# A two-block transformer kernel on one core: the latent edge of the MLA layer rebuilt, and the token reordering moved into the last chunks of the second feed-forward block

## The reference

```python
def _mla_mixer(h_lat, h_ctx, cos, sin, w_in, q_norm, kv_norm, w_uq, w_ukv, q_gain, k_gain, w_out, with_ctx_out):
    cq_l, ckv_l, kr_l = _split_cols(h_lat @ w_in, (512, 256, 32))
    ckv_c, kr_c = _split_cols(h_ctx @ w_in[:, 512:], (256, 32))
    k_l, v_l = keys_values(ckv_l, kr_l, True)     # rms, @ w_ukv, rms per head, rotary on the last 32
    k_c, v_c = keys_values(ckv_c, kr_c, False)
    q = queries(cq_l, True)                        # rms, @ w_uq, rms per head, rotary
    return attention(q, concat(k_c, k_l), concat(v_c, v_l)) @ w_out

xl = xl + mod_l[2] * y_lat
xl = xl + mod_l[5] * _conv_ffn(_modulate(xl, mod_l[3], mod_l[4]), ...)
# second block, first layer
h = rms_norm(x, norm_mix_pre[0], 1e-6)
m = hybrid_mixer(h, ...)    # differential and dilated window attention
```

## Time and profile before

| | us |
|---|---|
| median of 3 runs | 3988.12 (3987.25 to 3989.57) |
| profiled execution | 3985.7 |
| its span | 3983.7 |
| PE busy | 3752.9 (94%) |
| DVE busy | 1608.4 |
| ACT busy | 1514.2 |
| POOL busy | 1266.9 |

### The profile page before, as it was taken

How to read it: one execution, slowest core, us unless ns; L and a number is a source line. 1 busy time by engine, 2 the same in 40 slices (tenths; PEclk the granted TensorE clock), 3 DMA queues, 4 the chain that set the end, 5 groups by cost and what they waited for, 6 DMA issues and landing times.

```text
span 3983.7 us, 56653 instructions
## 1 busy us (share of the span) xinstructions
PE 3752.9 (94%) x21520; PEld 2948.7 (74%) x21520; DVE 1608.4 (40%) x2348; ACT 1514.2 (38%) x2528; POOL 1266.9 (32%) x524
## 2 busy tenths in 40 slices
PE   6998999999987989999979999989998999998998
PEld 3865678888865655788857778868876777876886
DVE  2423454242326664433355553331136555223113
ACT  3324442121245554322355553332235555333222
POOL 2530043222231010344522223434442222343443
PEclk9999999999998999999989999999999999999999
DMA  4344422111220000222311112222231211222232
GB/s 184 114 172 161 175 91 68 64 63 64 69 80 22 17 22 33 84 95 100 106 53 64 64 64 80 95 74 95 97 103 59 64 64 64 80 95 74 95 99 85
DMA packets 84717, 333.98 MB, mean 84 GB/s; under 512 B 9520, under 2 KB 9648, under 8 KB 78000
## 3 DMA queue, kind: packets, MB, share of 16 engines
q1 hardware_dynamic: 83808, 329.22, 24.3%
q10 hardware_dynamic: 720, 2.10, 0.2%
HBM read 329.18 MB, written 2.10 MB: 83 GB/s over the span
## 4 chain that ended last, share of the span: by engine, by line
PE 62%; issue 25%; POOL 5%; DVE 4%; ACT 2%; POOLq 0%; DVEq 0%; ACTq 0%
PE pB L2097 13%; PE pB L274 12%; PE pB L276 12%; PE pB L275 12%; POOL w_lo L2652 5%; PE pS L2127 1%; PE pT L2155 1%; PE pT L1706 1%; PE pB L1680 1%; PE pS L424 1%; PE pO L2177 1%; PE pO L2182 1%; PE pS L1697 1%; PE pO L276 1%; PE pO L274 1%
## 5 line engine op out<-in xcount | busy, mean ns | idle before, releaser
L2652 POOL TENSOR_TENSOR w_lo<-w_raw,w_hi 128x1024 fp32r<-128x1024 f32 x520 | 1266.7, 2437 | 2691.7 <-ACT w_hi L316 2691.1
L274 PE MATMUL pB<-h_hi,w_hi 128*128 128x512 f32 (+1 forms) x2112 | 839.1, 397 | 72.6 <-DVE h_lo L2581 20.1
L275 PE MATMUL pB<-h_lo,w_hi 128*128 128x512 f32 (+1 forms) x2112 | 830.1, 393 | 0.0
L276 PE MATMUL pB<-h_hi,w_lo 128*128 128x512 f32 (+1 forms) x2112 | 829.6, 393 | 0.0
L316 ACT ACTIVATE w_hi<-w_raw 128x1024 fp32r<-128x1024 f32 x520 | 547.6, 1053 | 477.8 <-PE pB L276 317.4
L274 PEld LDWEIGHTS pB<-h_hi,w_hi 128*128 128x128 f32 x2112 | 402.6, 191 | 174.8 <-issue 59.5
L276 PEld LDWEIGHTS pB<-h_hi,w_lo 128*128 128x128 f32 x2112 | 402.0, 190 | 85.1
L275 PEld LDWEIGHTS pB<-h_lo,w_hi 128*128 128x128 f32 x2112 | 402.9, 191 | 82.3 <-issue 0.5
L274 PE MATMUL pB<-b_hi,w_hi 128*128 128x512 f32 (+1 forms) x1088 | 399.7, 367 | 1.2 <-POOL w_lo L2652 0.9
L276 PE MATMUL pB<-b_hi,w_lo 128*128 128x512 f32 (+1 forms) x1088 | 397.2, 365 | 0.0
L275 PE MATMUL pB<-b_lo,w_hi 128*128 128x512 f32 (+1 forms) x1088 | 397.2, 365 | 0.0
(11 more groups left out here) (510 smaller groups left out, 5173.6 us busy)
## 6 DMA issues: line engine op xcount, KB each, us to landing
w_raw<-stream SPq DMA_DIRECT2D x520, 512.0 KB, 3.3
under<-ada SPq DMA_DIRECT2D x42, 1024.0 KB, 4.9
arena<-ada SPq DMA_DIRECT2D x6, 1024.0 KB, 18.8
x<-xT SPq DMA_DIRECT2D x1, 2048.0 KB, 10.1
out<-x SPq DMA_DIRECT2D x8, 256.0 KB, 2.0
xc<-cT SPq DMA_DIRECT2D x1, 1024.0 KB, 11.0
arena<-bmask ACTq DMA_DIRECT2D x1, 1024.0 KB, 4.8
arena<-brope ACTq DMA_DIRECT2D x2, 256.0 KB, 5.9
```

The source lines that it names most:

```text
L274: pe.matmul(dst, lh, rh, start=(begin and k == 0), stop=False)
L275: pe.matmul(dst, lh, rl, start=False, stop=False)
L276: last = pe.matmul(dst, ll, rh, start=False, stop=(end and k == len(pairs) - 1))
L2652: pool.tensor_tensor(w_lo[:, s, :], w_raw[:, s, :], w_hi[:, s, :].bitcast(F32), ALU.subtract).then_inc(lo_ready, 1)
```

## The change

Two edits at once.

1. MLA entry. The order of norms becomes `cq`, `ckv_lat`, `ckv_ctx`. The context norm is made by strips between the chunks 2 to 4; the squares and sums of `cq` lie around chunk 6, those of `ckv_lat` and `ckv_ctx` before and after the last context chunk. `act_mla_in` is one list of evacuations, squares, roots and hi tiles. `cq` goes to the upper half of pair B, and some buffers of the heads move between H and B; the attention outputs of pairs 4 to 7 go to H. In `FIRST_TURNS` Q and K of head 1 come before C, and PE waits for `ckv_ctx` only at C. In odd pairs the rotary step moves from step 4 to step 6 and the weight split from step 4 to step 5.

2. Reordering. In the last piece of the feed-forward block DVE writes residual plus old `x` to a buffer (`permuted_body`), ACT copies it with the stride into `x` and squares it for `mixpre0`, which becomes a norm by strips (`act_permute`, `pe_out_sums` through `sums="mixpre0"`). `dve_permute` and the norm's own squares and sums are gone.

```diff
-NORMS = [..., "cq", "ckv_ctx", "ckv_lat", "mla_ffn"]
+NORMS = [..., "cq", "ckv_lat", "ckv_ctx", "mla_ffn"]
-        STRIPS = ["ffn_lat", "ffn_ctx", "mla_lat", "mla_ffn"] + [...]
+        STRIPS = ["ffn_lat", "ffn_ctx", "mla_lat", "mla_ctx", "mla_ffn", "mixpre0"] + [...]
@@ pe_ffn / act_ffn / dve_ffn
+            sums = sums or post
...
-                if post is None or p + 1 < len(PIECES):
+                if p + 1 < len(PIECES):
                     act_out(act, g0 + 2 * nj)
+                elif post is None:
+                    act_permute(act, g0 + 2 * nj)
...
-                items(dve, KD, SLOTS, lambda m: out_body(p, g0 + 2 * nj, m))
+                if last_body is not None and p + 1 == len(PIECES):
+                    for m in range(KD):
+                        last_body(g0 + 2 * nj, m)
+                else:
+                    items(dve, KD, SLOTS, lambda m: out_body(p, g0 + 2 * nj, m))
@@ heads
-        hsq_q = [under[:, 2 + b, 6 * T:7 * T] for b in range(2)]
-        hsq_l = [under[:, 2 + b, 7 * T:8 * T] for b in range(2)]
+        hsq_q = [under[:, b, 6 * T:7 * T] for b in range(2)]
+        hsq_l = [under[:, b, 3 * T:4 * T] for b in range(2)]
-        q_src = (h_hi[:, 2 * TC:], h_lo[:, 2 * TC:])
+        q_src = (b_hi[:, KD * C:], b_lo[:, KD * C:])
+        def o_place(p):
+            return B if p < PAIRS_A // 2 else H
-        FIRST_TURNS = [("Q", 0), ("K", 0), ("C", 0), ("SQ", 0), ("SK", 0), ("SC", 0), ("Q", 1), ("K", 1), ("SQ", 1), ("SK", 1)]
+        FIRST_TURNS = [("Q", 0), ("K", 0), ("Q", 1), ("K", 1), ("SQ", 0), ("SK", 0), ("C", 0), ("SC", 0), ("SQ", 1), ("SK", 1)]
+                if turn == ("C", 0):
+                    pe.wait_ge(nlo_ready, norm_done("ckv_ctx"))
-                    if p + 1 < PAIRS_A and p % 2 and s == 4:
+                    if p + 1 < PAIRS_A and p % 2 and s == 5:
                         act_hi_part(act, g + 6)
-                        if s == (4 if p % 2 else 6):
+                        if s == 6:
                             dve_turn(dve, ("rotary", 2 * p + 3))
@@ pe_mla_in
-            pe_first_chunks(pe, G_MLA[0], 2, normed("mla_lat"), H, T, T)
-            pe_norm(pe, "mla_ctx", C)
-            items(pe, 5, SLOTS, lambda m: pe_chunk(pe, m + G_MLA[0], H, T, T), 2)
-            pe.wait_ge(nlo_ready, norm_done("mla_ctx"))
-            items(pe, 3, SLOTS, lambda m: pe_chunk(pe, m + G_MLA[1], B, C, C))
+            pe_first_chunks(pe, lat, 2, normed("mla_lat"), H, T, T)
+            pe_strip_sums(pe, "mla_ctx", 0, 4, C)
+            chunk(2)
+            pe_strip_sums(pe, "mla_ctx", 4, KD - 1, C)
+            chunk(3)
+            pe_strip_end(pe, "mla_ctx", C)
+            chunk(4)
+            chunk(5)
+            for kt in range(2):
+                pe_square_sum(pe, "cq", kt, T)
+            chunk(6)
+            for kt in range(2, 4):
+                pe_square_sum(pe, "cq", kt, T)
+            pe.wait_ge(nlo_ready, norm_done("mla_ctx"))
+            ctx_chunk(0)
+            ctx_chunk(1)
+            pe_norm(pe, "ckv_lat", T)
+            ctx_chunk(2)
+            pe_norm(pe, "ckv_ctx", C)
@@ act_mla_in
+            for kt in range(4):
+                act_strip_square(act, "mla_ctx", kt, tile_of(xc, C), C, ctx_in)
+            evacuate(0)
+            evacuate(1)
+            for kt in range(4, KD - 1):
+                act_strip_square(act, "mla_ctx", kt, tile_of(xc, C), C, ctx_in)
+            evacuate(2)
+            act_strip_part(act, "mla_ctx", C)
+            act_strip_square(act, "mla_ctx", KD - 1, tile_of(xc, C), C, ctx_in)
+            evacuate(3)
+            act_hi_part(act, g0 + 6)
+            act_root(act, "mla_ctx", C)
+            highs("mla_ctx", C, lambda kt: modc(1, 0, kt, 1), (*B, 0))
...
+            act.activation(places[4], bank[(g0 + 4) % SLOTS][:, 0:T], ACT.Copy).then_inc(evac[(g0 + 4) % SLOTS], 1)
+            for kt in range(2):
+                act_square(act, "cq", kt, tile_of(cq), T)
+            evacuate(5)
+            for kt in range(2, 4):
+                act_square(act, "cq", kt, tile_of(cq), T)
+            evacuate(6)
+            act_root(act, "cq", T)
+            highs("cq", T, None, (*B, KD * C))
+            evacuate(7)
+            for kt in range(2):
+                act_square(act, "ckv_lat", kt, lambda k: ckv[:, k, C:TC], T)
+            evacuate(8)
+            act_root(act, "ckv_lat", T)
+            highs("ckv_lat", TC, None, (*H, C))
+            evacuate(9)
+            for kt in range(2):
+                act_square(act, "ckv_ctx", kt, tile_of(ckv, C), C)
+            act_root(act, "ckv_ctx", C)
+            highs("ckv_ctx", TC, None, (*H, 0))
@@ reordering
-        def dve_permute(dve):
-            for kt in range(KD):
-                dve.wait_ge(perm_a, kt + 1)
-                dve.tensor_copy(x[:, kt, :], nt[:, kt % 3, :]).then_inc(perm_b, 1)
+        def permuted_body(dve):
+            def body(g0, m):
+                dve.wait_ge(chunk_done, done(g0 + m))
+                if m >= 3:
+                    dve.wait_ge(perm_b, m - 2)
+                dve.scalar_tensor_tensor(nt[:, m % 3, :], bank[(g0 + m) % SLOTS][:, 0:T], modc(1, 5, m, 0), x[:, m, :], ALU.mult, ALU.add
+                                         ).then_inc(evac[(g0 + m) % SLOTS], 1)
+            return body
+        def act_permute(act, g0):
+            act.preload_act_table_set(LN_EXP)
+            for m in range(KD):
+                act_hi_part(act, g0 + 2 + m)
+                if m == KD - 1:
+                    act_strip_part(act, "mixpre0", T)
+                act.wait_ge(*ev(g0 + m))
+                act.activation(x[:, m, :].rearrange("p (q j t) -> p q j t", q=TB, j=4),
+                               nt[:, m % 3, :].rearrange("p (q t j) -> p q j t", q=TB, j=4), ACT.Copy).then_inc(perm_b, 1)
+                act_strip_square(act, "mixpre0", m, tile_of(x), T, (perm_b, m + 1))
```

More of the change, by code:

```diff
@@ L280, in wt, with source @@
             return w_hi[:, s, kt * P + c0:kt * P + c1], w_lo[:, s, kt * P + c0:kt * P + c1]
+        def source(src, kt):
+            return src(kt) if callable(src) else src
         def rows(hi, lo, width, kt, c0, c1, base=0):
@@ L289, in pe_chunk @@
             pe_wait_chunk(pe, g)
-            pairs = [(wt(s, kt), rows(*src, width, kt, 0, n)) for kt in range(kts)]
+            pairs = [(wt(s, kt), rows(*source(src, kt), width, kt, 0, n)) for kt in range(kts)]
             if between is not None:
@@ L304, in pe_first_chunks @@
                     s = (g + e) % SLOTS
-                    last = pe_three(pe, bank[s][:, 0:n], [(wt(s, kt), rows(*src, width, kt, 0, n))], kt == 0, kt == kts - 1)
+                    last = pe_three(pe, bank[s][:, 0:n], [(wt(s, kt), rows(*source(src, kt), width, kt, 0, n))], kt == 0, kt == kts - 1)
                     if kt == kts - 1:
@@ L429, in pe_norm @@
                 pe_square_sum(pe, name, kt, n)
-        STRIPS = ["ffn_lat", "ffn_ctx", "mla_lat", "mla_ffn"] + [f"{w}{l}" for l in range(LAYERS) for w in ("mixpost", "ffnpre", "ffnpost")]
+        STRIPS = ["ffn_lat", "ffn_ctx", "mla_lat", "mla_ctx", "mla_ffn", "mixpre0"] + [f"{w}{l}" for l in range(LAYERS) for w in ("mixpost", "ffnpre", "ffnpost")]
         def pe_strip_sums(pe, name, k0, k1, n):
@@ L742, in pe_scaled_chunks, with pe_ffn @@
                         last.then_inc(chunk_done, 1)
-        def pe_ffn(pe, call, norm, n, width, post=None):
+        def pe_ffn(pe, call, norm, n, width, post=None, sums=None):
+            sums = sums or post
             for p, (j0, nj) in enumerate(PIECES):
@@ L1969, in pe_mla_in @@
         def pe_mla_in(pe):
[L1970 to L1974 removed]
+            lat, ctx_ = G_MLA
+            chunk = lambda j: pe_chunk(pe, lat + j, H, T, T)
+            ctx_chunk = lambda j: pe_chunk(pe, ctx_ + j, B, C, C)
@@ L1976, in act_mla_in @@
+            ctx_chunk(0)
[3 more added lines that the diff above has]
+            pe_norm(pe, "ckv_ctx", C)
         def act_mla_in(act):
             r = slice(NOPE, P)
-            dsts = [cq[:, j, :] for j in range(4)] + [ckv[:, j, C:TC] for j in range(2)] + [kraw[0][r, C:TC]]
-            for g0, n, ds_ in ((G_MLA[0], T, dsts), (G_MLA[1], C, [ckv[:, j, 0:C] for j in range(2)] + [kraw[0][r, 0:C]])):
-                for j, dst in enumerate(ds_):
-                    if j or g0 != G_MLA[0]:
-                        act_hi_part(act, g0 + j + 2)
-                    act.wait_ge(chunk_done, done(g0 + j))
-                    rows_ = r if j == len(ds_) - 1 else slice(0, P)
-                    act.activation(dst, bank[(g0 + j) % SLOTS][rows_, 0:n], ACT.Copy).then_inc(evac[(g0 + j) % SLOTS], 1)
@@ new lines, in act_mla_in, with evacuate, highs @@
+            places += [ckv[:, j, 0:C] for j in range(2)] + [kraw[0][r, 0:C]]
+            g0 = G_MLA[0]
+            def evacuate(j):
+                g = g0 + j
+                n = T if j < 7 else C
+                rows_ = r if j in (6, 9) else slice(0, P)
+                if j:
+                    act_hi_part(act, g + 2)
```

(7 more changed lines are left out.)

47 lines of the change are left out of this document (18 added, 29 removed).

## The result

The changed kernel took 3932.8 us (median of 4 runs, 3931.8 to 3933.4) against 3987.68 us for the kernel before (median of 4, 3982.6 to 3989.6): a ratio of 0.9862, with a 95% interval of 0.9846 to 0.9877. The time moved by 54.9 us where the sum had 49.6, and it lies inside the range. The page has the span and the busy time of each engine; PE has 4 instructions more than in the earlier trace rows and is busy for 20.6 us less, and its idle time fell by 33.1 us (230.8 to 197.7). Of the 20.6 us of busy time some 16 are low clock, by an estimate from the two traces (PE's busy time times the share of the clock that was not granted: 60.7 us in before, 44.7 in after). The rest is work: two norms have strips where they had full sums, and the lines that make sums of squares are busy for 77.8 us in place of 89.6, in part at the lower clock.

A forecast was written before the change was run, and what follows sets the result against it. TensorE, busy 94% of the span, was taken as the bound, with time to win only where it idles or runs at its lower clock. Terms -22.3 + 6.2 - 16.8 - 16.7 = -49.6 us gave 3938 us, range 3925 to 3953.

The forecast's parts named there:

- Part 1: MLA entry input chunks: norms spread between the chunks bring the last norm tile earlier; gain 22.3 us, bounds 19 to 25.
- The rival in which ACT becomes the bound: Input chunks: ACT's single queue holds PE up, gain 12 in place of 22.3 us, total 3948; chance 0.10.
- Part 2: First turns of the heads: Q1 and K1 before C0 delay heads 0 and 1; loss 6.2 us.
- bound of 8: First turns: the bad end of the forecast loss, 8 us; the good end was 3.
- Part 3: Odd pairs of the heads: rotation in step 6 and split in step 5 remove PE's stall; gain 16.8 us, bounds 12 to 19.
- The rival in which the stall moves with the rotation: Odd pairs: DVE's step 7 copy comes after the query projection, saving 6 in place of 16.8 us, 3949; chance 0.08.
- The passage on the port: Splits beside two-SBUF-tensor DVE products: they exclude each other for a whole instruction; with shared bandwidth the total is 3 to 4 us lower.
- Part 4: End of the second feed-forward block: residual, copy and square lie under the next chunk; gain 16.7 us, bounds 14 to 18.
- The cover: Same block end: per-tile work takes 5.9 of 8.2 us before the weight is due, 2.2 to spare; failing, 3946, chance 0.05.
- the rival in which the new turn order costs nothing: First turns: the chain's tail shortens more than counted, so no loss, total 3932; chance 0.10.

The follow-up runs named there:

- after_again: The changed kernel run once more, unedited, on the same chip as the last follow-up; 3935.36 us (0.9867).
- warm_both: Changed kernel plus eight matmuls nobody reads in PE's first-turn pauses, five before Q1's product and three before the first score; 3927.53 us (one run).
- split_moved_only: Changed kernel with the odd pairs' rotation put back to step 4, the weight split still in step 5; 3948.06 us (one run).
- early_key: Changed kernel with the old turn order, and the shared key squared and rotated before the context key norm; 3921.83 us (0.9838).
- rotary_moved_only: Changed kernel with the odd pairs' weight split put back to step 4, the rotation still in step 6; 3934.3 us (one run).
- reorder_only: Kernel before with only the token reordering moved under the last output chunks and its norm by strips; 3969.32 us (0.9951).
- entry_only: Kernel before with only the norms between the input chunks changed; turn order, odd-pair steps and permutation as before; 3962.52 us (0.9934).
- warm_pe: Changed kernel plus five matmuls nobody reads on PE ahead of Q1's product; 3934.61 us (0.9870).
- steps_only: Kernel before with only the odd pairs changed, rotation in step 6 and weight split in step 5; 3965.18 us (0.9941).
- best: early_key with the third heads chunk's split behind the first query and the odd pairs' split back in step 4; 3919.8 us (0.9829).

## Why the prediction was right, and which term of it was off

**Part 1, right: 22.3 forecast, 23.2 measured** (23.6 in `after_again`). Counted from the entry, the order laid out by hand holds to about 1.3 us at each step. Shifted by the 2.53 us by which the entry began earlier: the context norm's root was put at 1153.7 and came at 1155.0; ACT was to be free of its tiles at 1162.6 and was at 1163.0; the `cq` tiles at 1178.8 and 1179.5; PE's pause at 2.4 and 2.2; the two latent tiles at 1187.1 and 1187.1; the last tile at 1193.5 and 1192.7. The last is where the extra gain lies: I priced the last sums at 2.05 us after a pause of 3.8, from the earlier trace rows, and they took 1.43 after 2.86. The rival in which ACT becomes the bound had a granted clock of 1.00 and no pause against it.

**Part 2, mis-sized: a loss of 6.2 forecast, 9.1 measured, beyond its bound of 8.** This is the step that failed. Its mechanism was right: the chain through K1 puts head 0 at +18.0 where I had +17.1, and the 0.9 us are Q1 and K1 out of PE at the lower clock, 6.9 us after Q0 in place of 6.1. The other 2.0 us lie between head 0 and head 1. The prediction said that "the later part of the chain, score, maximum, exponential" is the same for head 1, and took its durations from a stretch at a granted clock of 1.00. In the new order PE pauses 3.10 us right ahead of the scores, and they run at its lower level of 1.2 GHz: 11.1 us from head to head in after, 9.08 in `warm_both` (the 9.1 that I had used). The estimate by the traces' clock gives the same: between head 0 and head 1 PE lost 2.05 us to the lower clock in after, none in before or in `warm_both`. With the fillers the loss at the value product is 4.6 us, so about half of the 9.1 is the clock and half the chain. The bound of 8 had the clock in the products that I had moved and not in those behind them.

**Part 3, right: 16.8 forecast, 17.7 measured** (6.42, 4.98 and 6.34 against 6.1, 4.6 and 6.1). The wait of 1.1 us that I put into step 5 came as 0.84, by the cause that I gave (ACT's copy behind its split), and the margin that I gave the last copy, 0.8 us, was 0.44. Both halves of the old stall are now shown, the queue order by `split_moved_only` and the stretching by the difference to the earlier trace rows. The rival in which the stall moves with the rotation had only that margin against it; it held in all three pairs. What I had not drawn from my own wait is that moving the split bought nothing: I took over the pair of edits as one. With the split in step 4 that wait is gone and each odd pair is 0.93 us shorter.

The passage on the port went the way of the rule. In before, in after and in `early_key` a DVE product of two tensors in SBUF that takes 0.68 us alone took 2.73 to 2.80 beside a split, which is what the Trainium skill, "SBUF — State Buffer", section "SBUF: two separate sides", says of such a pair: the second waits until the first is through. The ends show it as well. In all three kernels the product ended 0.54 to 0.56 us after the split (1315.00 against 1314.46 in before), so nearly all of it was done behind the split. Shared bandwidth would have added some tenths. Not every DVE operation is held: in `rotary_moved_only` a copy (1301.56) and a maximum (1300.46) that read PSUM ran beside the split of 1300.18 in 0.56 and 0.94 us, what they take elsewhere. And the hold goes both ways: the split of 1298.91 in after, with two-tensor products of DVE right at its start, took 2.84 us where 2.44 is its mean.

**Part 4, right: 16.7 forecast, 16.9 measured** (`reorder_only`; after has 18.0 in that stretch, 1.1 us of it from elsewhere). Two terms were off and cancel. The strips and their end put 2.8 us between the chunks (31.10 us from the first residual to the eighth, 28.34 before), not 2.1. The end took 8.15 us, not 8.9: the split was nearer its end when DVE's first product came, whose two records took 2.00 us, 0.6 more than the 1.41 of the same two in before, not 1.3 (the split ended 0.78 us after the product's start). The cover held: with no strips between them the residuals stand 4.08 us apart, the pace of PE.

**The sum.** The terms were wrong by +0.9, -2.9, +0.9 and +0.2 us; that makes -0.9. The difference to the forecast is thus not one of the parts: 49.6 forecast, 48.7 by the four parts, 53.7 between the spans, of which 2.5 us arose ahead of the changed code, and the other 2.4 us are spread behind it: 0.1 in the pairs, 1.1 before the second block and 1.2 in it. These are shorter spells at the lower clock, by the same estimate of what PE lost to it: 9.8 us ahead of the entry in after and 12.8 in before, 22.5 and 23.7 in the second block, and in the stretch before it 1.9 in after and 3.0 in `reorder_only`, which has the same edit there. Why the spells were shorter no run shows. So it is luck that the total, with part 2 short by 2.9 us, moved further than forecast and not less. It is luck too that 3932.8 meets the 3932 of the rival in which the new turn order costs nothing: the order cost 7.6 us. The four parts add up: alone they gave 23.6, 17.7 and 16.9 us at their own places, together 23.2, 17.7 and 18.0 (1.1 of it clock); the turns cost 7.6 by their order and 1.5 by the clock behind the earlier entry, which `entry_only` shows as 1.4.

## What to carry to other kernels

When a reordering puts a pause ahead of TensorE work that lies on the critical chain, price that work, and what follows it up to the next long busy stretch, at the lower clock, not only the work that was moved. When two steps are moved at once, ask of each alone what it does, and in whose queue it now stands first; here one half of the pair carried the gain and the other, a split ahead of a copy that PE wanted, took some of it back, and one line of the turn order cost 7.6 us inside a change that won 55. Compare traces by distances between events from the last common point, since totals hide parts of two or three microseconds behind the drift of what comes before.

## What the hardware showed that I had not expected

**Behind the same pause the low-clock spell is there in one kernel and missing in another with the same code at that place, and a gain can vanish into that.** PE pauses 2.45 us before the value product of pair 6 in both kernels (1543.45 in before); in after the row is

```profile
1508.98 0.61 PE L1695 MATMUL pB<-arena 128*64 128x512 f32 x1 [2.45 <-ACT attT L1767]
```

From there to the next value product it took 27.54 us in before and 25.84 in after, and the stretch behind it 33.90 and 35.60: the same sum, with 1.7 us of low clock on one side or the other. The clock shows it: over the 6 us from the value product of pair 6 the granted clock is 0.72 in before and 1.00 in after, and from that of pair 7 it is 1.00 and 0.72. In `warm_pe` it is 0.72 behind both, 27.54 and 35.52 us, which ate the filler's gain; in `steps_only` the distances are 25.83 and 35.54. `after_again` has 25.83, as after, so the two profiles of one kernel agree here. Nothing in the profiles that I read says which it will be. That stays open, and I read no effect under 2 us from a total of this kernel.

**The last norm's sums ran at either clock.** The same four sums took 2.04 us behind a pause of 4.63 us in `best`, 1.43 behind 2.86 in after and 1.10 behind 3.27 in `early_key`. So the length of the pause alone doesn't order them; what does was not tried.

**Filler matmuls can pay.** Eight matmuls whose result nobody reads brought the first value product 4.46 us earlier. One run of 3927.53 us against 3935.36 for the changed kernel on that chip points the same way. `best` reaches more without fillers: with the old turn order its longest pause of PE between Q0 and head 1 is 1.82 us.
